# Picks built from the places, contiguous low rows, and the last expert pair's down product by column halves, in a fused two-block transformer kernel

## The reference, cut to what matters

```python
def _hierarchical_moe(u, rg_w, rg_b, re_w, re_b, wg, wu, wd):
    ...
    g_logits = (t @ rg_w + rg_b).astype(jnp.float32)
    g_prob = jax.nn.softmax(g_logits, axis=-1)
    g_idx = jnp.argmax(g_logits, axis=-1)
    ...
    e_logits = jnp.take_along_axis(e_all, g_idx[:, None, None], axis=1)[:, 0]
    top_v, top_i = lax.top_k(e_logits, TOP_K_IN_GROUP)
    weights = g_w * jax.nn.softmax(top_v, axis=-1)
    ...
    def run_block(args):
        e, tok, w = args
        xb = t[tok]
        hid = jax.nn.silu(xb @ wg[e]) * (xb @ wu[e])
        return ((hid @ wd[e]).astype(jnp.float32) * w[:, None])
    ...
    y = jnp.zeros((n, D), jnp.float32).at[slot_tok].add(outs.reshape(n_slots, D))

h = h + _hierarchical_moe(_rmsnorm(h, norm_ffn_w[l]), ...)
return _rmsnorm(h, norm_final_w)
```

## Time and profile before

| | |
|---|---|
| median of 3 runs | 1331.71 us (1331.38 to 1332.31) |
| the profiled execution, its own time | 1332.89 us |
| its span | 1331.1 us |
| busy: PE, VectorE (DVE), ScalarE (ACT) | 1283.1, 589.4, 470.9 us |
| granted TensorE clock, mean | 0.991 |
| read from HBM, written | 347.05 MB, 1.05 MB |

### The profile page before, as it was taken

The page is one execution under the profiler, slowest core; times in us unless marked ns, Lnnn a source line. Parts: engine busy times, 40 slices in busy tenths (PEclk is TensorE's granted clock), DMA queues, the critical chain, the costliest instruction groups (busy, mean ns, idle before and its releaser), DMA issues.

```text
span 1331.1 us, 19137 instructions
## 1 busy us (share of the span) xinstructions
PE 1283.1 (96%) x8326; PEld 969.4 (73%) x8326; DVE 589.4 (44%) x939; ACT 470.9 (35%) x698; POOL 64.8 (5%) x68
## 2 busy tenths in 40 slices
PE   8999999999999999999999999999999999999996
PEld 7886798999998989979999999834344343443432
DVE  3576656444556587485655556622011110111112
ACT  4543555334454644444554554321011010110102
POOL 4021000000000121010010000000000000000000
PEclk9999899999999999999999999999999999999999
DMA  9786433766544534443445549489999999999995
GB/s 353 273 281 235 148 125 114 249 210 190 182 126 153 165 125 159 148 161 127 129 149 190 189 161 370 198 327 421 420 421 420 421 421 421 420 421 420 421 421 211
DMA packets 102548, 349.35 MB, mean 262 GB/s; under 512 B 6114, under 2 KB 9472, under 8 KB 77888
## 3 DMA queue, kind: packets, MB, share of 16 engines
q1 hardware_dynamic: 100912, 345.56, 68.5%
q0 software_dynamic: 1376, 2.50, 0.8%
q10 hardware_dynamic: 176, 0.07, 0.0%
HBM read 347.05 MB, written 1.05 MB: 262 GB/s over the span
## 4 chain that ended last, share of the span: by engine, by line
PE 82%; DVE 7%; DMA 6%; ACT 4%; issue 1%; DVEq 0%; ACTq 0%
PE bank L551 43%; PE bank L933 14%; PE bank L968 7%; DMA weights<-in_expert_w_up 4%; PE bank L785 3%; PE bank L744 2%; DVE WHL L1406 2%; DMA arena<-in_expert_w_up 2%; PE bank L578 2%; PE bank L474 2%; PE bank L508 2%; ACT WHL L987 1%; PE bank L518 1%; PE bank L685 1%; PE bank L711 1%
## 5 line engine op out<-in xcount | busy, mean ns | idle before, releaser
L551 PE MATMUL bank<-XH,WHL 128*128 128x256 f32 x2928 | 542.2, 286 | 8.1 <-DVE WHL L1406 3.9
L551 PEld LDWEIGHTS bank<-XH,WHL 128*128 128x128 f32 x2928 | 463.2, 193 | 14.5 <-issue 7.9
L551 PE MATMUL bank<-XL,WHL 128*128 128x256 f32 x1464 | 415.8, 284 | 0.0
L1406 DVE TENSOR_TENSOR WHL<-weights,WHL 128x1024 fp32r<-128x1024 f32 x223 | 282.8, 1285 | 216.1 <-ACT WHL L987 215.7
L987 ACT ACTIVATE WHL<-weights 128x1024 fp32r<-128x1024 f32 x223 | 232.0, 1054 | 212.0 <-PE bank L551 206.7
L551 PEld LDWEIGHTS bank<-XL,WHL 128*128 128x128 f32 x1464 | 283.1, 193 | 0.1
L933 PE MATMUL bank<-arena 128*64 128x512 f32 x512 | 142.3, 593 | 2.6 <-DMA arena<-in_expert_w_up 2.6
L933 PE MATMUL bank<-weights,arena 128*64 128x512 f32 x384 | 113.6, 593 | 5.1 <-DMA weights<-in_expert_w_up 5.1
L551 PE MATMUL bank<-WHL,XH 128*128 128x512 f32 x320 | 105.1, 403 | 4.1 <-DVE WHL L1406 4.1
L933 PEld LDWEIGHTS bank<-arena 128*64 128x64 f32 x512 | 45.7, 137 | 72.0 <-issue 67.1
L2107 DVE SCALAR_TENSOR_TENSOR chainm<-bank,small,chainm 128x512 f32<-128x512 f32 x16 | 12.0, 751 | 183.1 <-PE bank L933 183.1
(11 more groups left out here) (347 smaller groups left out, 1244.5 us busy)
## 6 DMA issues: line engine op xcount, KB each, us to landing
weights<-in_w_in SPq DMA_DIRECT2D x58, 1024.0 KB, 5.1
arena<-in_expert_w_gate SPq DMA_DIRECT2D x32, 1024.0 KB, 19.8
arena<-in_expert_w_up SPq DMA_DIRECT2D x32, 1024.0 KB, 23.0
arena<-in_expert_w_down SPq DMA_DIRECT2D x32, 1024.0 KB, 26.1
weights<-in_expert_w_up SPq DMA_DIRECT2D x24, 1024.0 KB, 24.8
weights<-in_expert_w_down SPq DMA_DIRECT2D x24, 1024.0 KB, 24.5
weights<-in_expert_w_gate SPq DMA_DIRECT2D x24, 1024.0 KB, 20.6
weights<-in_w_ada SPq DMA_DIRECT2D x22, 1024.0 KB, 7.5
```

The source lines that it names most:

```text
L551: ins = e.matmul(o, l, r, start=first, skip_group_check=True, stop=g.part == g.parts - 1 and k == g.kc - 1 and n == 2)
L1406: e.tensor_tensor(lo, unit_weights(g, u), hi, ALU.subtract).then_inc(S.w_lo, 1)
```

## The change

It has four parts.

1. **Picks.** `ph` is multiplied with the choice of experts 0 to 3 (`dv[:, :, 0:4]`) in one operation of 1024 elements into `direct`, which lies in the buffer `y_even`; one addition of 512 elements over the two ranks writes the whole `pick` of group 0. The eight operations of `slots_of` for pairs 0 and 1 go, and `inpair` moves behind `chosen(0)`. Semaphore counts follow (`picked`, `weighed`, `RT_EG`, `RT_E2`).
2. **Unread products.** `spin(7, 32)` becomes `spin(7, 15)`.
3. **Low rows.** ScalarE makes two more copies of the tokens, reordered by chunk but not rounded, into `full`; `low_rows` then reads and writes in one run.
4. **Last pair.** `last_down` computes the down product for `n = 0` with both experts, then `n = 1` for expert 0, `weigh(0)` (the two combine products of column half 0), `n = 1` for expert 1, and `weigh(1)`. The four last loads hold column halves (4 rows of 2 KB to a partition) where they held `k` halves. Squares go to idle buffers (`junk`), and the end goes through (0, 0), (1, 0), (0, 1), (1, 1).

```diff
@@ -284,6 +284,7 @@
         hp = [chainm[:, i * HID:(i + 1) * HID] for i in range(2)]
         hpT = [maskf[:, i * HID:(i + 1) * HID].rearrange("p (k s) -> p k s", k=4) for i in range(2)]
         uTe = hT
+        junk = hp + [maskf[:, i * HID:(i + 1) * HID] for i in range(2)]
         def col(name, k=0):
             r = ROWS[name] + k
@@ -777,13 +778,39 @@
             def combine(p):
                 w.wait_ge(S.m_wc, p + 1)
                 for i in range(4):
-                    n, j = divmod(i, 2) if p < NPAIR - 1 else (i % 2, i // 2)
+                    n, j = divmod(i, 2)
                     w.wait_ge(S.m_ya if n else S.m_yv, p + 1)
                     b = 2 * j + n
                     if p == 0:
                         clear(b)
                     e.matmul(bank[b][:, :], wpT[p % 2][:, j * P:(j + 1) * P], yo[p % 2][n],
-                             start=p == 0, stop=p == NPAIR - 1, skip_group_check=True).then_inc(S.m_cb, 1)
+                             start=p == 0, stop=False, skip_group_check=True).then_inc(S.m_cb, 1)
+
+            def last_down():
+
+                p = NPAIR - 1
+
+                def product(n, ss_):
+                    clear(6 + n)
+                    for k in range(4):
+                        for s_ in ss_:
+                            x = moe_load(p, 2, n, s_)
+                            w.wait_ge(*moe_landed(x))
+                            ins = e.matmul(bank[6 + n][64 * s_:64 * s_ + 64, :], hpT[p % 2][:, k, 64 * s_:64 * s_ + 64],
+                                           moe_weights(x, 4, HID)[:, k, :], start=k == 0, stop=k == 3)
+                    ins.then_inc(S.m_dn, 1)
+
+                def weigh(n):
+                    w.wait_ge(S.m_ya if n else S.m_yv, p + 1)
+                    for j in range(TT):
+                        e.matmul(bank[2 * j + n][:, :], wpT[p % 2][:, j * P:(j + 1) * P], yo[p % 2][n], start=False,
+                                 stop=True, skip_group_check=True).then_inc(S.m_cb, 1)
+                w.wait_ge(S.m_wc, p + 1)
+                product(0, (0, 1))
+                product(1, (0,))
+                weigh(0)
+                product(1, (1,))
+                weigh(1)
             w.wait_ge(S.d_ident, 32)
@@ -918,7 +945,7 @@
             free[6] = (S.posc, 1)
-            spin(7, 32)
+            spin(7, 15)
             choose(0)
             for p in range(NPAIR):
                 for wi in range(2):
@@ -957,6 +984,9 @@
                 if p % 2 and p + 1 < NPAIR:
                     choose(p // 2 + 1)
                 w.wait_ge(S.m_hc, p + 1)
+                if p == NPAIR - 1:
+                    last_down()
+                    break
                 for k in range(4):
                     half, kk = divmod(k, 2)
                     for n in range(2):
@@ -970,7 +1000,6 @@
                             if kk == 1:
                                 ins.then_inc(S.m_dn, 1)
                 free[6], free[7] = (S.m_yv, p + 1), (S.m_ya, p + 1)
-            combine(NPAIR - 1)
         def scalar(e):
@@ -1341,6 +1370,9 @@
             for j in range(TT):
                 e.activation(by_chunk(uhi)[:, j, :, :], xtok2[:, j, :].rearrange("p (q k) -> p q k", k=KC),
                              ACT.Copy).then_inc(S.rn, 1)
+            for j in range(TT):
+                e.activation(by_chunk(full)[:, j, :, :], xtok2[:, j, :].rearrange("p (q k) -> p q k", k=KC),
+                             ACT.Copy).then_inc(S.rn, 1)
             w.wait_ge(S.d_late, LATE)
             w.wait_ge(S.rp, 1)
             w.wait_ge(S.rt, RT_DPOS)
@@ -1375,21 +1407,20 @@
                 if p % 2 and p + 1 < NPAIR:
                     slot_norms(p // 2 + 1, 6)
                     chosen(p // 2 + 1)
-                w.wait_ge(S.m_dn, 8 * p + 8)
+                w.wait_ge(S.m_dn, 8 * p + (8 if p < NPAIR - 1 else 3))
                 if p >= 2:
                     w.wait_ge(S.m_cb, 4 * (p - 1))
                 e.activation(yo[p % 2][1], bank[7][:, :], ACT.Copy).then_inc(S.m_ya, 1)
-            for j in range(TT):
-                for n in range(2):
-                    i = 2 * j + n
-                    w.wait_ge(S.acc, i + 1)
-                    e.activation(yo[0][n], xtok2[:, j, n * 512:(n + 1) * 512], ACT.Square,
-                                 accum_out=small[:, 44 + i:45 + i]).then_inc(S.sq, 1)
-                w.wait_ge(S.ss, NORMS + j + 1)
-                sj = small[:, 34 + j:35 + j]
-                e.activation(sj, sj, ACT.Sqrt, bias=epsc[:, 0:1], scale=1.0 / D).then_inc(S.rms, 1)
+            for i, (j, n) in enumerate(HALVES):
+                w.wait_ge(S.acc, i + 1)
+                e.activation(junk[i], xtok2[:, j, n * 512:(n + 1) * 512], ACT.Square,
+                             accum_out=small[:, 44 + 2 * j + n:45 + 2 * j + n]).then_inc(S.sq, 1)
+                if i >= 2:
+                    w.wait_ge(S.ss, NORMS + j + 1)
+                    sj = small[:, 34 + j:35 + j]
+                    e.activation(sj, sj, ACT.Sqrt, bias=epsc[:, 0:1], scale=1.0 / D).then_inc(S.rms, 1)
             w.wait_ge(S.d_late, LATE)
@@ -1996,11 +2027,8 @@
                 then(e.tensor_tensor(onehot, onehot, tmp1.broadcast_to([P, TT, n]), ALU.is_equal))
             def low_rows(j):
-                w.wait_ge(S.rn, j + 1)
-                e.tensor_tensor(ulo[:, j, :].rearrange("p (k q) -> p k q", k=KC),
-                                xtok2[:, j, :].rearrange("p (q k) -> p k q", k=KC),
-                                uhi[:, j, :].bitcast(F32).rearrange("p (k q) -> p k q", k=KC),
-                                ALU.subtract).then_inc(S.rl, 1)
+                w.wait_ge(S.rn, TT + j + 1)
+                e.tensor_tensor(ulo[:, j, :], full[:, j, :], uhi[:, j, :].bitcast(F32), ALU.subtract).then_inc(S.rl, 1)
             gl = lg[:, :, 0:4]
             first_max(gl, 4, goh, gmax)
@@ -2035,14 +2063,17 @@
             then(e.tensor_tensor(ph, iota.unsqueeze(1).broadcast_to([P, two, CAP]),
                                  place.broadcast_to([P, two, CAP]), ALU.is_equal))
             last()
-            then(e.tensor_tensor(inpair, ph.unsqueeze(2).broadcast_to([P, two, 2, CAP]),
-                                 par.unsqueeze(3).broadcast_to([P, two, 2, CAP]), ALU.mult))
+            then(e.tensor_tensor(direct, ph.unsqueeze(2).broadcast_to([P, two, 4, CAP]),
+                                 dv[:, :, 0:4].unsqueeze(3).broadcast_to([P, two, 4, CAP]), ALU.mult))
             last()
-            for p in range(2):
-                slots_of(p, pick[:, :, p * P:(p + 1) * P], pair)
+            by_rank = direct.rearrange("p (j r) e s -> p j r (e s)", r=2)
+            e.tensor_tensor(pick[:, :, :], by_rank[:, :, 0, :], by_rank[:, :, 1, :], ALU.add).then_inc(S.m_slots, 1)
+            nslots[0] += 1
             for j in range(TT):
                 low_rows(j)
             chosen(0)
+            then(e.tensor_tensor(inpair, ph.unsqueeze(2).broadcast_to([P, two, 2, CAP]),
+                                 par.unsqueeze(3).broadcast_to([P, two, 2, CAP]), ALU.mult))
             then(e.tensor_tensor(eg, gl, gmax.broadcast_to([P, TT, 4]), ALU.subtract))
             assert nr[0] == RT_EG
             then(e.tensor_tensor(e2, m2, m1, ALU.subtract))
@@ -2112,7 +2143,7 @@
                     weigh_over()
                 if p % 2 and p + 1 < NPAIR:
                     chosen(p // 2 + 1)
-                w.wait_ge(S.m_dn, 8 * p + 8)
+                w.wait_ge(S.m_dn, 8 * p + (8 if p < NPAIR - 1 else 1))
                 if p >= 2:
                     w.wait_ge(S.m_cb, 4 * (p - 1))
                 e.tensor_copy(yo[p % 2][0], bank[6][:, :]).then_inc(S.m_yv, 1)
@@ -2120,11 +2151,11 @@
             def added(j, n):
                 o = xtok2[:, j, n * 512:(n + 1) * 512]
-                w.wait_ge(S.m_cb, 4 * (NPAIR - 1) + 2 * j + n + 1)
+                w.wait_ge(S.m_cb, 4 * (NPAIR - 1) + HALVES.index((j, n)) + 1)
                 e.tensor_tensor(o, bank[2 * j + n][:, :], o, ALU.add).then_inc(S.acc, 1)
             def summed(j):
-                w.wait_ge(S.sq, NORMS * KC + 2 * j + 2)
+                w.wait_ge(S.sq, NORMS * KC + j + 3)
                 e.tensor_tensor(small[:, 34 + j:35 + j], small[:, 44 + 2 * j:45 + 2 * j], small[:, 45 + 2 * j:46 + 2 * j],
                                 ALU.add).then_inc(S.ss, 1)
@@ -2137,9 +2168,8 @@
                     c = slice(n * 512, (n + 1) * 512)
                     e.scalar_tensor_tensor(out=normed[:, j, c], in0=xtok2[:, j, c], scalar=sj, in1=frow[:, c],
                                            op0=ALU.mult, op1=ALU.mult).then_inc(S.t_out, 1)
-            added(0, 0)
-            added(0, 1)
-            added(1, 0)
+            for j, n in HALVES[0:3]:
+                added(j, n)
             summed(0)
             added(1, 1)
             scaled(0)
@@ -2271,6 +2301,10 @@
                                 w.wait_ge(*moe_ring[x][2])
                             else:
```

(14 more changed lines are left out.)

## The result

The changed kernel took 1335.28 us (median of 8 runs, 1334.38 to 1336.32) against 1330.83 for the kernel before (8 runs, 1329.60 to 1332.31), a ratio of 1.0034, 95% interval 1.0023 to 1.0044: about 4.5 us **slower**. The forecast was 1332.2, 1329.8 to 1334.2, with "within 0.2%" as the likely case. It was wrong. The profiled execution took 1335.64, with a span of 1334.0; before that was 1332.89 and 1331.1.

The account below looks back on a forecast made before the run. The prediction saw three stages: router (TensorE, VectorE), a fixed-rate stream of loads, and a dependent chain at the end. Head -3.80 plus end +4.25 gave +0.45 us, on the median 1331.71 a forecast of 1332.2, range 1329.8 to 1334.2.

Parts of the forecast that it names:

- Spin, picks, low rows, gather, stream: Router: shorter spin and picks end together; gather starts 3.80 us earlier, carried through the load stream to the last product.
- The 2 KB rows: Last four loads: 386 GB/s against 421, so 10.9 us instead of 10.0, hidden.
- The end: From the last down product's start to the last scaled row: 20.15 us instead of 15.90, 4.25 longer.
- the lost pairing: Last down product, experts apart: four products alone cost about 3.43 us, like four pairs; 3.4 us of the loss.
- the norm's order: Last normalisation: both tiles now wait for column half 1, adding 0.85 us.
- Sum: Whole kernel: -3.80 at the head plus 4.25 at the end, +0.45 us.
- Case 2: Gather: the shorter spin only uncovers another wait, the head's gain is lost, +4.25 us, 1336.0; chance 0.07.
- Cases 1, 3, 4 and 5: Halves alone run fast, 1328.7, 0.10; last loads late, 1335.1, 0.04; end cheaper otherwise, 0.08; lower clock, 1336, 0.02.
- Chance: Whole kernel: 0.79 within 0.2%, 0.10 faster, 0.11 slower; the forecast's own case had 0.69.

Follow-up runs that it names:

- the last two kernels: Changed kernel with experts paired again and 30 unread products in TensorE's waits: 1327.26 us with the changed norm order, 1325.89 us with the old one.
- the pair without the guard: Kernel before and changed kernel, both without the overflow flag's reading, its branches and the skipped recomputation: 1330.46 us and 1331.07 us.
- head_fill17: Kernel before with the changed router (picks, low rows, 15 unread products) and 17 unread products put back in TensorE's waits: 1328.21 us, ratio 0.9973.
- picks_only: Kernel before with the new picks, ScalarE's two copies and contiguous low rows, keeping its 32 unread products and its end: 1331.74 us, ratio 1.0001.
- spin_only_fill17: Kernel before with 15 unread products instead of 32 ahead of the gather, and 17 put back in later waits: 1330.49 us, ratio 0.9991.
- tail: Kernel before, its router kept, with the changed end (column halves, experts apart, new norm order): 1338.45 us, ratio 1.0048.
- after_fill17: Changed kernel with 17 unread products put back where TensorE waits: 1335.22 us, ratio 1.0024; the same kernel once more, 1335.06 us, ratio 1.0025.
- run 22: Not a label: the text says the kernel before was run 22 times, unchanged; those runs spread over 6.0 us.

## Why the prediction was wrong, step by step

- *Spin, picks, low rows, gather, stream.* Right. `direct` took 1.23 (forecast 1.22), a low row 1.18 (1.22), the shift was 3.80 beside the 0.47 that was there before, and it reached the last product whole. Clock 1.00 as forecast. The 2 KB rows, alone in the stretch 1300 to 1304 us, moved 387 GB/s, where the kernel before moved 422 in 8 KB rows, close to the prediction's 386 against 421; they were hidden.
- *The end.* Right: 20.22 us for 20.15, though two misses cancel in it. `weigh(1)` started at 13.26 and not at 13.01, and the normalisation behind it took 6.96 and not 7.14 (`added(1, 1)` came 0.08 behind `summed(0)`, not 0.23). Taken apart by the last two kernels, its terms were less well placed than its total: splitting the experts costs 4.5 (the 3.4 of the lost pairing, the 0.9 of the last copy, which `weigh(0)` no longer covers, and 0.2 more), the norm's order 0.7 for the 0.85 forecast, and column half 0 first gives 0.9 back, a term that the prediction did not name: 4.3.
- *Sum.* This is the step that failed: "-3.80 + 4.25 = +0.45 us. The profiled execution, 1332.89, would become 1333.3". It carried what stands behind the last scaled row, 1331.1 - 1328.95 = 2.1 us, over as it was. So it put the closing branch at no change without a reason. The missing term is TensorE's part of that branch, 475 ns before and 3352 after, +2.9; with it the sum is 3.3 us, and 1332.89 + 3.3 = 1336.2 for a profiled execution that took 1335.64 (and was 0.47 ahead before any edit), or 1330.83 + 3.3 = 1334.2 for a median that was 1335.28. The lower end of the ratio's interval is 1333.9, so the 1.1 us that are left lie within the noise, and no run gives them a cause. The sum without the branch was measured: +0.6 in the pair without the guard.
- *Rivals.* Case 2, the head swallowed, gave 1336.0, close to the result for a reason that is not there: its mark, the gather waiting past 859.5, is absent, and `head_fill17` has the gain. Cases 1, 3, 4 and 5 did not happen either. No case held the mechanism that did; in the page of the profile nothing draws the eye to it, since a branch isn't counted as busy and the chain's shares are the same in both.
- *Chance.* 0.79 on "within 0.2%" rested on the sum's terms, each from a row, and left nothing for a term that is not in the diff's lines: the number of instructions ahead of a branch.

**What stays open.** That the branch is short when a q8 fetch was made 38 to 83 TensorE instructions ahead of it, and long when the last was 208 or more ahead, holds in all profiled executions above; where the border lies is not known. What sets the moment of the fetch at the margin does not follow from a count alone. The kernel before, `head_fill17`, `picks_only` and `spin_only_fill17` have 16851 TensorE instructions and the old end, and all fetch with 53 to 57 left. `tail` and the two executions of `after_fill17` have the same count and the changed end, and only one of the three fetched, with 38 left. So the changed end moves the fetch later. That the waits for copies between the last products, which only that end has, keep TensorE's sequencer from running ahead is argued and was not tested.

## What to carry to other kernels

Read the trace to its last line and subtract: a span that differs while the last arithmetic ends at the same time points to what stands behind it, here a branch that nobody edited. If a kernel ends in a guard that jumps over code, instructions added or removed ahead of it can move a code fetch across it, so compare variants of such a kernel with the guard's branch time beside them, or with the guard out of both; a difference of 3 us can be that alone. And where products of half the width run in pairs, an order that separates the partners pays the full time of a pair for each.

## What the runs showed that I had not expected

A branch of TensorE that is taken over code took 0.37 to 0.48 us where the fetch had been made, and 3.35 to 3.97 where it had not, while that of VectorE took 67 ns in both kernels. The same program can do either from one execution to the next, as the two traces of `after_fill17` show. The spread of the times alone would not have told it: its eight runs spread over 5.0 us, but the kernel before, run 22 times beside it, spread over 6.0. Unread work where TensorE waits anyway can therefore make a kernel faster: 30 products more are worth 0.4% to the changed kernel.
